# A diffusion backbone step on one core: the prompt block's experts put behind the sample's projections and into the sample's attention

## What is computed

```python
h = rms_norm(x, norm1_g) * (1 + sc1) + sh1
z = h @ w_in                                  # q, k, v of two attentions, gate logits
o_g = gqa_attention(q_g, k_g, v_g); o_d = diff_attention(q_d, k_d, v_d, lam)
merged = gate_a * (o_g @ w_branch_a) + gate_b * (o_d @ w_branch_b)
x = x + g1 * (merged @ w_out)
h2 = rms_norm(x, norm2_g) * (1 + sc2) + sh2
# experts (PEER): 8 heads, each picks 16 of 16384 experts for each token
idx, wts = top16(h2 @ w_query against sub_keys)
a = gelu(einsum('nd,nhkd->nhk', h2, peer_u[idx]))       # 128 dots a token
x = x + g2 * einsum('nhk,nhkd->nd', a * wts, peer_v[idx])   # 128 rows summed a token
```

## Time and profile before

| what | value |
|---|---|
| median of 3 runs | 5433.13 us (5430.0 to 5439.07) |
| profiled execution | 5433.29 us, span 5431.6 us |
| mean granted clock of PE | 0.741 |
| PE busy | 3269.6 us (60%) |
| DVE busy | 2984.2 us (55%) |
| moved by DMA | 1893.16 MB, mean 349 GB/s |

### The profile page before, as it was taken

How to read it: one execution, slowest core, us unless ns; L and a number is a source line. 1 busy time by engine, 2 the same in 40 slices (tenths; PEclk the granted TensorE clock), 3 DMA queues, 4 the chain that set the end, 5 groups by cost and what they waited for, 6 DMA issues and landing times.

```text
span 5431.6 us, 31813 instructions
## 1 busy us (share of the span) xinstructions
PE 3269.6 (60%) x10286; PEld 1284.2 (24%) x10286; DVE 2984.2 (55%) x4043; ACT 425.4 (8%) x793; POOL 1896.5 (35%) x1354
## 2 busy tenths in 40 slices
PE   5486979999454577789999376000333333333566
PEld 0043434444333433344444133000000000000000
DVE  1231014788798623167667784999665565565200
ACT  0011000000122200011001010000000000000000
POOL 0000002355333101034444442566554544544333
PEclk7797989999677788999999688555555555555566
DMA  9985877799877488699999997898999999999998
GB/s 390 395 314 176 290 257 270 272 380 368 331 282 275 155 331 332 247 381 373 357 372 341 395 355 279 328 370 355 421 418 418 418 418 421 419 418 418 418 415 367
DMA packets 414157, 1893.16 MB, mean 349 GB/s; under 512 B 30294, under 2 KB 33910, under 8 KB 243022
## 3 DMA queue, kind: packets, MB, share of 16 engines
q0 software_dynamic: 186848, 1347.98, 61.5%
q1 hardware_dynamic: 227184, 543.72, 27.1%
HBM read 1850.33 MB, written 42.57 MB: 348 GB/s over the span
## 4 chain that ended last, share of the span: by engine, by line
DMA 39%; PE 33%; DVE 20%; issue 5%; POOL 2%; ACT 1%; SPq 0%; DVEq 0%; POOLq 0%; PEldq 0%; ACTq 0%
PE ps L665 26%; DMA activations<-in_peer_v,zt 21%; DVE big L1620 5%; DMA big<-in_peer_v,zt 4%; DVE big L1339 4%; DMA big<-in_w_ada 4%; DVE big L1329 2%; DMA big<-in_peer_v,sel 2%; DMA big<-in_peer_u,sel 2%; PE ps L931 2%; POOL big L617 1%; PE ps L785 1%; DMA big<-in_w_branch_a 1%; DVE work L1286 1%; PE ps L693 1%
## 5 line engine op out<-in xcount | busy, mean ns | idle before, releaser
L665 PE MATMUL ps<-big,activations 128*128 128x512 f32 x4096 | 1804.8, 601 | 103.6 <-DMA big<-in_w_out 29.4
L1620 DVE CUSTOM_DVE_ANT_0 big<-big,activations 128x2048 f32<-128x2048 f32 x384 | 867.3, 2289 | 502.6 <-DMA big<-in_peer_u,sel 501.1
L665 PEld LDWEIGHTS ps<-big,activations 128*128 128x128 f32 x4096 | 781.3, 192 | 1112.8 <-issue 1035.7
L648 POOL DMA_INDIRECT big<-in_peer_u,sel x384 | 567.3, 1477 | 577.3 <-DVE zt L1620 505.2
L1329 DVE CUSTOM_DVE_ANT_0 big<-big 128x2048 f32<-128x2048 f32 x256 | 581.2, 2291 | 211.9 <-DMA big<-in_peer_u,sel 167.8
L617 POOL DMA_INDIRECT big<-in_peer_v,sel x256 | 453.9, 1773 | 669.9 <-DVE big L1339 530.4
L617 POOL DMA_INDIRECT big<-in_peer_u,sel x256 | 418.7, 1635 | 729.2 <-DVE work L1329 608.3
L1339 DVE SCALAR_TENSOR_TENSOR big<-big,work 128x2048 f32<-128x2048 f32 x256 | 601.9, 2351 | 119.6 <-DMA big<-in_peer_v,sel 111.3
L931 PE MATMUL ps<-activations 128*32 128x512 f32 x1536 | 359.3, 1028 | 452.9 <-DMA activations<-in_peer_v,zt 452.9
L931 PE MATMUL ps<-big,activations 128*32 128x512 f32 x1536 | 350.7, 1007 | 432.5 <-DMA big<-in_peer_v,zt 429.7
L606 POOL DMA_DIRECT2D work<-scores x40 | 23.9, 597 | 856.3 <-DMA scores<-zone 791.6
(11 more groups left out here) (171 smaller groups left out, 2036.1 us busy)
## 6 DMA issues: line engine op xcount, KB each, us to landing
big<-in_w_in SPq DMA_DIRECT2D x84, 2048.0 KB, 10.3
big<-in_w_ada SPq DMA_DIRECT2D x48, 2048.0 KB, 12.1
big<-in_w_out SPq DMA_DIRECT2D x24, 2048.0 KB, 11.1
big<-in_peer_w_query SPq DMA_DIRECT2D x24, 2048.0 KB, 9.9
big<-in_w_branch_a SPq DMA_DIRECT2D x12, 2048.0 KB, 19.6
big<-in_w_branch_b SPq DMA_DIRECT2D x12, 2048.0 KB, 8.5
big<-z_blocks SPq DMA_DIRECT2D x20, 512.0 KB, 12.2
big<-in_peer_u,sel POOLq DMA_INDIRECT x640, 10.8
```

Source lines behind the costliest of these rows:

```text
L648: pool.indirect_dma_start(u_slot(m), None, eu, bass.IndirectOffsetOnAxis(ap=sel[:, t % 2, k:k + 1], axis=0)).then_inc(u_in[m % UR], 16)
L665: ins = nc.tensor.matmul(bank(bk), acts[:, k, b * P:(b + 1) * P], w[:, n % WS, k], start=(start and k == 0), stop=(stop and k == KT // 2 - 1))
L1620: V.tensor_tensor_reduce(out=x, in0=x, in1=h_of[ph], scale=1.0, scalar=0.0, op0=ALU.mult, op1=ALU.add, accum_out=dots_b[ph % 2][:, st * TO ...
```

## The change

The prompt block's experts take another form, and no step of them is left behind the branches.

- All 128 dots (`dot`) stand behind the 36 units of the sample's projections, 3 or 4 after each, and `choose` of steps 1 to 7 after dots 4, 20, ... 100. Weights, indices and dots of all steps are kept in `zone`.
- After the last dot the indices are turned on PE, copied by DVE, and POOL gathers peer_v by token over the same ring of 4. ACT takes one gelu over 128 columns, DVE one product with the weights, PE turns the coefficients, and ACT spreads them in quarters of 32 tokens (`spread_quarter`).
- PE sums a token with 4 matmuls (`token`) into bank 7: tokens 0 to 15 (`EARLY`) between the turns of keys 2, 3 and 4, then two in each score step: 32 in each of blocks 0 to 2 and 16 in block 3. The tokens stand after the turn of the weights and ahead of the output.
- Bank 7 was one of two output banks. Outputs of the sample's attention now have one (`out_bank`), and PE waits for DVE's scaling of the output before. Bank 2 takes the place of bank 7 for queries.
- DVE copies a finished quarter (`sums`) in the middle of each block, SP stores it to `v_sums`, and `acc` is loaded from there (1 MB) before the sub-keys of g = 1. `final` runs where step 7 ended.
- PE's loop over attention blocks is written out, as is POOL's loop of the prompt's gathers. The semaphores of later stages count on from there, and some that were used once are merged.

```diff
+EARLY = 16
...
+        idx_0, wts_0, dots_0, coef_0, coef_t0, idx_f0 = [zn(3328 + P * i, P) for i in range(6)]
+        idx_t0 = idx_f0.bitcast(u32)
+        spread_0 = [bg(G0 + 4 * D + 1024 * i, 1024) for i in range(2)]
+        sum_0 = ac(A1 + 7680, CH)
...
+        QBANK = (4, 5, 6, 2)
...
+        def out_bank(p, o):
+
+            return 6 if p else 6 + o % 2
+
+        def dots_behind(x):
+
+            return range(x * P // (QKV_CH * SB), (x + 1) * P // (QKV_CH * SB))
+
+        def choice_behind(m):
+
+            return m // TOPK + 1 if m % TOPK == 4 and m // TOPK + 1 < PH else None
+
+        def tokens_behind(b, sc):
+
+            first = EARLY + 32 * b + 2 * sc
+            return range(first, min(first + 2, P))
...
+            def sums_out(q):
+
+                sp.wait_ge(sum_ok, q + 1)
+                for j in range(NQ):
+                    sp.dma_start(vsd[32 * q:32 * q + 32, j * CH:(j + 1) * CH], sum_0[32 * j:32 * j + 32]).then_inc(sum_st, 16)
...
+                        sp.wait_ge(sum_st, 16 * NQ * NQ)
+                        sp.dma_start(acc, vsd).then_inc(fa_in, 16)
...
+                if g == 0:
+                    for t in range(PH):
+                        pool.wait_ge(sel_ready, t + 1)
+                        if t + 1 < PH:
+                            scores_in(t + 1)
+                        for k in range(TOPK):
+                            m = t * TOPK + k
+                            pool.wait_ge(ring_free, m + 1)
+                            pool.indirect_dma_start(slot(m), None, eu, bass.IndirectOffsetOnAxis(ap=sel[:, t % 2, k:k + 1], axis=0)).then_inc(ring_in[m % RING], 16)
+                    pool.wait_ge(idx_t_ok, 1)
+                    for n in range(P):
+                        m = P + n
+                        pool.wait_ge(ring_free, m + 1)
+                        pool.indirect_dma_start(slot(m), None, ev, bass.IndirectOffsetOnAxis(ap=idx_t0[:, n:n + 1], axis=0)).then_inc(ring_in[m % RING], 16)
...
+                def token(n):
+
+                    q, i, m = n // 32, n % 32, P + n
+                    if i == 0:
+                        pe.wait_ge(spread_ok, q + 1)
+                        if q:
+                            pe.wait_ge(vq_free, q)
+                    pe.wait_ge(ring_in[m % RING], 16 * (m // RING + 1))
+                    for j in range(NQ):
+                        ins = nc.tensor.matmul(ps[32 * j:32 * j + 32, 7 * 512:8 * 512], spread_0[q % 2][:, i * 32:(i + 1) * 32],
+                                               slot(m)[:, j * CH:(j + 1) * CH], start=(i == 0), stop=(i == 31))
+                    ins.then_inc(ring_free, 1)
+
+                if p:
+                    pe.wait_ge(idx_ok, 1)
+                    nc.tensor.transpose(bank(7, P), idx_0, ident[:, :]).then_inc(idx_tr, 1)
...
+                    if p and t == 1:
+                        pe.wait_ge(idx_t_ok, 1)
+                        pe.wait_ge(coef_ok, 1)
+                        nc.tensor.transpose(bank(7, P), coef_0, ident[:, :]).then_inc(coef_tr, 1)
+                    if p and t >= 2:
+                        for n in range((t - 2) * EARLY // 3, (t - 1) * EARLY // 3):
+                            token(n)
...
-                with pe.Fori(0, blocks) as i:
+                for i in range(blocks):
...
-                        if o >= 2:
+                        if p:
+                            pe.wait_ge(a["oe"], qb * 12 + o + 2)
+                        elif o >= 2:
...
-                            if o:
-                                output(o - 1)
+                        if p:
+                            for n in tokens_behind(i, sc):
+                                token(n)
+                        if o:
+                            output(o - 1)
...
-                    if p and c in QKV_STEPS:
-                        top_exps(QKV_STEPS[c] + 1)
-                        gelus(0, QKV_STEPS[c] * 2 * TOPK)
+
+            def spread_quarter(q):
+
+                if q >= 2:
+                    sa.wait_ge(ring_free, RING + P + 32 * (q - 1))
+                nc.scalar.activation(spread_0[q % 2][:, 0:1024:33], coef_t0[:, 32 * q:32 * q + 32], ACT.Copy).then_inc(spread_ok, 1)
...
+                    if p and t == 1:
+                        sa.wait_ge(ring_free, RING + P)
+                        nc.scalar.activation(coef_0, dots_0, ACT.Gelu).then_inc(ge_done, 1)
+                        sa.wait_ge(coef_tr, 1)
+                        nc.scalar.activation(coef_t0, bank(7, P), ACT.Copy).then_inc(coef_t_ok, 1)
+                        sa.wait_ge(coef_t_ok, 1)
+                        spread_quarter(0)
+                        spread_quarter(1)
...
-                        if p and sc == gelu_score(i):
-                            if i + 1 < blocks:
-                                top_exps(i + 5)
-                                gelus(0, (i + 4) * 2 * TOPK)
+                        if p and sc == 10 and i < 2:
+                            spread_quarter(i + 2)
...
-                c = 0
-                while c < QKV_CH:
-                    if p and c in QKV_STEPS:
-                        step = QKV_STEPS[c]
-                        peer_step(0, step, step % 2, step, during=lambda k: unit(c * n + k // 4) if k % 4 == 3 else None)
-                        c += 2
-                    else:
-                        for lb in range(n):
-                            unit(c * n + lb)
-                        if p == 0 and c % 2 == 0 and c < 2 * SB:
-                            norm(nrm[3], 3, c // 2 + 1, 0)
-                        c += 1
+                for c in range(QKV_CH):
+                    for lb in range(n):
+                        unit(c * n + lb)
+                        if p:
+                            for m in dots_behind(c * n + lb):
+                                dot(m)
+                                if choice_behind(m):
+                                    choose_0(choice_behind(m))
+                    if p == 0 and c % 2 == 0 and c < 2 * SB:
+                        norm(nrm[3], 3, c // 2 + 1, 0)
+                if p:
+                    dve.sem_inc(idx_ok, 1)
+                    dve.wait_ge(idx_tr, 1)
+                    V.tensor_copy(idx_t0, bank(7, P)).then_inc(idx_t_ok, 1)
+                    dve.wait_ge(ge_done, 1)
+                    V.tensor_tensor(coef_0, coef_0, wts_0, ALU.mult).then_inc(coef_ok, 1)
+
+            def dot(m):
+
+                dve.wait_ge(ring_in[m % RING], 16 * (m // RING + 1))
+                V.tensor_tensor_reduce(out=slot(m), in0=slot(m), in1=hcur, scale=1.0, scalar=0.0, op0=ALU.mult, op1=ALU.add,
+                                       accum_out=dots_0[:, m:m + 1]).then_inc(ring_free, 1)
+
+            def choose_0(step):
+
+                lo = step * TOPK
+                choose(step, step % 2, wts_0[:, lo:lo + TOPK], idx_0[:, lo:lo + TOPK])
+
+            def sums(q):
+
+                dve.wait_ge(ring_free, RING + P + 32 * (q + 1))
+                if q:
+                    dve.wait_ge(sum_st, 16 * NQ * q)
+                ins = V.tensor_copy(sum_0, bank(7))
+                ins.then_inc(sum_ok, 1)
+                dve.wait_ge(sum_ok, q + 1)
+                dve.sem_inc(vq_free, 1)
...
-                    if p and b < 3:
-                        peer_step(0, b + 4, b % 2, b + 4, during=behind)
-                    else:
-                        if b:
-                            out(10, qb - 1)
-                            out(11, qb - 1)
-                            end(qb - 1)
-                        for i in range(17):
-                            item(i)
+                    if b:
+                        out(10, qb - 1)
+                        out(11, qb - 1)
+                        end(qb - 1)
+                    for i in range(17):
+                        item(i)
+                        if p and i == 9:
+                            sums(b)
...
-                elif g == 1:
-                    peer_step(0, 7, 1, 7, ahead=False, during=lambda k: merge(k // 8) if k % 8 == 7 else None)
-                    dve.wait_ge(fa_in, 48)
-                    final(ac(A1 + 2 * D, D), ac(A1 + 3 * D, D), ac(A1, D), 1)
+                    if g:
+                        dve.wait_ge(fa_in, 64)
+                        final(ac(A1 + 2 * D, D), ac(A1 + 3 * D, D), ac(A1, D), 1)
```

114 lines of the change are left out of this document (54 added, 60 removed).

## The result

The change takes 5387.9 us (median of 4 runs, 5383.4 to 5390.1) against 5431.6 of the kernel before in the same comparison (5424.3 to 5439.1): a ratio of 0.992 with a 95% interval of 0.9908 to 0.9932, or 44 us less. I had forecast 5358 and 5295 to 5425: inside the range, the right sign, and 60% of the gain. The profiled execution took 5383.4 us, its span 5381.8, 49.8 less than that of before.

A forecast was written before the change was run, and what follows sets the result against it. It took PE to bound the projections, DVE the attention blocks, and gathers' bandwidth to slow the branches. Projections 0, to the attention's end −25 (10 from the handover) and branches −50 took 5433.3 to 5358 us, range 5295 to 5425.

The forecast's parts named there:

- Step 1: Sample's projections: DVE's extra choices fit behind PE's products, PE ends at 1376.5 as before; price 0, from −8 to +15.
- DVE behind PE at the end of the projections (step 1): Projections: a sign listed as showing the forecast wrong, with no time given.
- Step 2: Handover from projections to attention: last dots near 1390, first output at 1450, −10 us, bounds −22 and +10.
- V, which the sum had as its term: Handover: V's load, taken as 24 us instead of 34, sets the first output at 1450.
- Step 3: Attention blocks: 5.9 us a score step, 109 instead of 129 for a block with 32 tokens.
- the round of four slots: Attention blocks: the gather ring's round of 11.6 us, 2.9 a token, sets the score step.
- The single output bank: Attention blocks: costs nothing in the sum; without tokens, waits of some tenths of a us in 4 outputs.
- Step 4: Branches after the attention: −17 to the first product and −33 in the products, together −50, ends −35 and −60.
- The attention's −25: Attention's end at 1851 instead of 1875.9, 10 of the gain from the handover; ends −84 and +16.
- B: Rival, attention blocks: PE's clock falls, blocks take about 160 us, total 5557; with weaker forms, chance 0.09.
- A: Rival, attention blocks: gathers keep up and PE sets the step; attention ends at 1792, total 5299; chance 0.12.
- C: Rival, no net change: 6.6 us a step, V as before, branches give only 35; total 5424; chance 0.09.

The follow-up runs named there:

- e1: The change, with ACT copying the next unit's bank before the exponentials of choices 1 to 4: 5374.5 us, ratio 0.9888 to the kernel before.
- e11: The change, with five ring slots instead of four for the dots' gathers in the prompt block: 5372.6 us, ratio 0.9888 to the kernel before.
- e10: The change, with 16 of the 128 dots not computed but their gathers kept: 5378.3 us in one run.
- e4: The change, with PE turning all five keys before it waits for the indices, early tokens after: 5397.9 us, ratio 0.9936 to the kernel before.
- e14: The change, with 30 of a quarter's 32 tokens multiplied by one matmul over 32 columns, all gathers and waits kept: 5379.0 us in one run.
- e7: The change, with 32 gathers of peer_u, read by no engine, put back beside the branches: 5443.3 us, ratio 1.0017 to the kernel before.

## Why the prediction was right in its sign and wrong in its size

**Step 1, the projections, failed.** It said: "the lag is gone before the last chunk", "PE therefore ends where it did", price 0 from −8 to +15. PE ended 26 us later. The first half came true: DVE had caught up before the last two chunks and waited for ACT there.

```profile
1327.25 0.43 DVE L1347 COPY zone<-zt 128x512 f32<-128x512 f32 x1 [12.41 <-ACT zt L1014]
```

The "therefore" is the step that failed. While DVE lags by more than PE's banks hold, PE stands, and in a stage that PE limits this time is not won back when DVE has caught up: PE's three waits sum to 31 us up to 1144, where 8.4 stood, and from 1180 on PE has no idle time in which to make them up. The working also took the choices as work spread over 36 units and compared means (DVE 16.4, ring 11.5, PE 13.8). But a choice comes in one piece of 12 us, in which the ring stands full and, through ACT's exponential, PE's banks stand too. e1 shows ACT's part, e11 and in part e10 the ring's. The rival named as a sign ("DVE behind PE at the end of the projections (step 1)") is what the trace shows, but I had given it no price.

**Step 2, the handover, failed.** "The last dots end near 1390 (four at 3.25)": it is 14 dots that stand behind units which PE finishes only from 1382.7 on, and DVE ended the last one at 1427. With step 1 that makes a key turn 41 us late, and 35 later than forecast. The path to the first output was wrong as well: it came at 1497.6, not at 1450, and it did not wait for V, which the sum had as its term. Behind the last key turn (1462.8) came six tokens whose gathers PE waited for, up to the queries at 1480.4, and then the 17 us of queries and exponentials. "SP loads queries and V only behind that turn" was right and did not matter (e4).

**Step 3, the blocks, was right in size:** 109 forecast, 102 measured for blocks 1 and 2; block 3 91 and 90.3; block 0 from its first output 92 and 85. Together that is 21 us less than the sum had, and it is luck for the total: the first output came 48 us later than in the sum, the attention's end 26 later. 5.9 us a step was near the mark, but the reason was not the round of four slots: with 25 us less work on PE the blocks did not shrink (e14), and the steps run at nearly the full rate of the DMA with a pause of about 22 us at the block's change. PE's busy 82 and its clock of 0.95 or more were as said. The single output bank cost what was said, tenths of a us at a time: six waits for DVE's scaling (L1533), 3.9 us over the four blocks.

**Step 4, the branches, was right:** −17 and −33 forecast, −17.1 and −36.9 measured, and e7 gives the cause. The attention's −25 did not come at all (+1.3), and the time is inside the range because that range was wide enough for a forecast without it.

**Rivals.** B did not come. In the blocks PE waited for gathers 30 times in 307 us, and the granted clock stayed at 0.95 to 0.97. Where tokens stand alone, in the key stage, it was 0.66, and the same eight records took 1.94 us instead of 1.06. The Trainium skill's "TensorE: Matmul & The Clock Gate" says, in its section on how the oscillation bites in real kernels, that matmuls which come in groups with waits for transfers between them start each group on a slowed clock; the trace bears this out in that stage with its 0.66 and not in the blocks with their 0.95 to 0.97, where other matmuls fill the time between waits. In e14, where PE waited 39 us for gathers in the same two blocks instead of 20, it was 0.82. A fell with e14. C named the attention as the place where the gain is lost, and that is where it was lost, but not through its terms: neither the round trip nor V did it, and the branches gave 54 us, not its 35.

## What to carry to other kernels

Work that comes in one piece, a choice of 12 us between streamed operations, should be set against the buffers of each stream that it stops, not averaged over the stage: a ring of four slots hides four gathers and no more. Where the engine that limits a stage is held for a while, that time is lost, also if the one that held it catches up later. Where a following stage waits for the last piece of a stream, count what hangs behind the last input of the producer, not the stream's mean pace. And before moving gathers, find where the transfers are already at the chip's rate: 32 of them cost 60 us beside weight loads (e7), 1.9 us each, and 16 of them 25 us in the last attention block, 1.6 each; neither place was free.

## What the runs showed of the hardware that I had not expected

- Matmuls of 32 output rows at four places of the array run side by side so fully that one takes as long as four: 71.0 and 68.7 us for 64 tokens, 1.1 us each.
- Those narrow matmuls do not hold PE's clock down where others stand between them (0.95), but alone, waiting for gathers, they run near half of it (0.66 in the key stage; 1.94 us a token instead of 1.06).
- Work taken away from PE can come back as a lower clock: with the tokens narrowed to 32 columns (e14) the granted clock of blocks 1 and 2 is 0.82 instead of 0.96, and of 49 us saved 24 are lost in the other matmuls.
- A ring of four 1 MB gathers reaches 350 to 430 GB/s in most slices of the score steps; the eight and eight slots of the last phase reach 418 to 421.
